# Strassen down projection: other places for the activations' sums, and low parts of plain weight blocks made by an accumulating DMA

## The chip, the cores and the metric

One NeuronCore of a Trainium2 chip runs the whole kernel in one launch. TensorE (PE) multiplies, PEld is its weight load, VectorE (DVE) and ScalarE (ACT) do elementwise work, GpSimd (POOL) does a little more of it, and SyncE (SP) issues the DMAs. The metric is the device time of one execution in microseconds, lower is better. Before the change it is 2497.34 us, the median of three runs (2496.92 to 2497.78).

## What is computed

```python
def swiglu(x, w_gate, w_up, w_down):
    return (jax.nn.silu(x @ w_gate) * (x @ w_up)) @ w_down

for layer in range(2):
    h = h + 0.5 * swiglu(rms_norm(h, norm_ffn1[layer]), ...)
    hn = rms_norm(h, norm_mix[layer])
    h = h + (even_mixer(hn, ...) if layer % 2 == 0 else fourier_mixer(hn, ...))
    h = h + 0.5 * swiglu(rms_norm(h, norm_ffn2[layer]), ...)
return rms_norm(h, norm_final)[:, N_META:]
```

The model width is 1024, the feed-forward width D_FF = 2816. There are 528 + 272 = 800 tokens (two sequences, 16 meta tokens before each). All is float32. Four feed-forward networks (f = 0 to 3) are most of the work: f = 0, the even mixer (attention and pooling), f = 1, f = 2, the odd mixer (a Fourier transform), f = 3.

## The kernel before, in words

**Split products.** A float32 operand is held as a high part (rounded to fp32r) and a low part (the rest), and a product is three matmuls: high by high, high by low, low by high (L1983 to L1985 in gate and up, L2056 to L2058 in down). A weight block of 128x512 is a *unit*: ACT writes its high part (L805) into one of NS = 6 slots, DVE subtracts it from the source and writes the low part (L1215) into the same slot of `w_lo`. A unit's slot is free when PE has done unit n - 6 (`unit_done`).

**Strassen.** Gate, up and most of down are done by Strassen's scheme in Winograd's form: seven products P1, P5, P6, P3, P7, P2, P4 (in this order) in place of eight. Their weights are A11, S1, S2, S4, S3, A12, A22. The four S are sums that DVE makes (L1199 to L1207) from the quarters in `raw`, which SP loads by DMA (a ring of six quarters, 256 KB each); the three A are quarters as they are. Each product is one unit of 12 matmuls. Their right sides are the *forms* B11, T1, T2, B22, T3, B21, N4, with T1 = B12 - B11, T3 = B12 - B22, T2 = B22 - T1, N4 = B21 - T2.

**Chunks.** D_FF is 22 tiles of 128, in chunks of 4, 4, 4, 4 and 6. For each of the first four chunks PE does the gate and up products of its tiles (seven units each; the first two tiles of a network, the lead, are done plainly), and then its down projection in two groups g = 0, 1 of seven units (`down_group`). This change of stage, from the last gate and up unit of a chunk to its first down unit, occurs 4 x 4 = 16 times and is called the *transition* here. The last chunk and the mixers' projections are plain (L1904, L1897).

**The activations.** DVE multiplies up by silu(gate) into `act32` (L1404, L1415), makes the sums T1, T3, T2, N4 there (L1429), ACT writes their high parts (L914) to `act_hi`, DVE their low parts (L1439) to `act_lo`. `act32` and `act_lo` are the same memory, by places 0 to 6 (`ACT_AT`): each low part overwrites the float32 form at its own place, so it waits until the last sum that reads that form is made. B22, T2 and T3 stand side by side and get their high and low parts in one instruction of three forms, which waits for N4; and N4 needs B21, which needs the up half P4, the last gate and up unit of the chunk. For the last tile of a chunk the product is made in halves (L1415): first B22's (half 1), later B21's (half 0).

**The order** of each engine is written out by hand in `ffn`. Between its other steps an engine calls `weights_to(k)`: ACT makes high parts up to unit k + 4, DVE low parts up to k + 3 and sums up to two further. After each half of a down product DVE adds PSUM to `h` (`down_adds`, L1464); PE waits for that add before it accumulates on the same bank again. POOL has nothing to do in a network but one small power (`rstd`). SP's load over an old quarter waits for that quarter's last low part and last sum.

## Time and profile before

| | |
|---|---|
| median of three runs | 2497.34 us |
| the profiled execution | 2500.72 us, of which the span from its first to its last instruction is 2498.9 us |
| PE busy | 2404.6 us, 96% |
| DVE busy | 1987.6 us, 80% |
| ACT busy | 1087.5 us, 44% |
| POOL busy | 80.0 us, 3% |
| DMA | 169.68 MB, one queue of 22.7% of 16 engines |

Busy times are sums of recorded durations; matmuls overlap (they start every 0.18 us and each is recorded as 0.34 us long), so PE's share says only how seldom it stood still. The page's span is 1.8 us shorter than the execution.

### The profile page before, as it was taken

What the parts mean: (1) busy time and instruction counts of PE and PEld (TensorE: products, weight loads), DVE (VectorE), ACT (ScalarE), POOL (GpSimd) and SP (SyncE); (2) the same over time, 40 slices, a digit from 0 to 9 for tenths busy, and PEclk for the clock granted to TensorE, in tenths of its full rate; (3) what the DMA queues carried; (4) which work ended last, traced back from release to release, by engine and by line L of the source; (5) the groups of instructions that cost most, each with busy time, mean ns of one, the idle gap of its engine ahead of it and who ended that gap; (6) DMA issues with size and microseconds to landing.
All of it is one profiled execution on the core that took longest, in us unless ns stands there. A gap on an engine that the chain in (4) does not pass through costs nothing.

```text
span 2498.9 us, 36765 instructions
## 1 busy us (share of the span) xinstructions
PE 2404.6 (96%) x13364; PEld 2348.6 (94%) x13364; DVE 1987.6 (80%) x3664; ACT 1087.5 (44%) x2028; POOL 80.0 (3%) x86
## 2 busy tenths in 40 slices
PE   9999999999999999999999999999999999999998
PEld 8899999999579999999999999999989899999997
DVE  8988988753746988978768897897755898898876
ACT  6453453431743443443444344344443544344353
POOL 0000000006000000000000000000012100000000
PEclk9999999999999999999999999999999999999999
DMA  3222222222011222222221222222221222222223
GB/s 122 68 68 68 68 68 68 72 88 72 18 30 51 60 68 68 66 69 65 68 72 51 68 59 68 68 62 68 76 72 45 78 62 68 70 66 73 70 68 122
DMA packets 92338, 169.68 MB, mean 68 GB/s; under 512 B 10624, under 2 KB 23296, under 8 KB 92032
## 3 DMA queue, kind: packets, MB, share of 16 engines
q1 hardware_dynamic: 92160, 167.34, 22.7%
q8 instruction: 108, 1.77, 0.3%
q14 instruction: 70, 0.57, 0.1%
HBM read 164.02 MB, written 3.28 MB: 67 GB/s over the span
## 4 chain that ended last, share of the span: by engine, by line
PE 76%; DVE 16%; issue 6%; ACT 1%; DMA 0%; POOL 0%; DVEq 0%; SPq 0%; POOLq 0%; ACTq 0%
PE banks L1904 13%; PE banks L1984 12%; PE banks L1985 12%; PE banks L1983 12%; PE banks L2056 6%; PE banks L2058 6%; PE banks L2057 6%; PE banks L2002 3%; PE banks L1897 3%; DVE w_lo L1215 3%; DVE act_lo L1439 2%; DVE act L1429 1%; DVE w_sum L1207 1%; DVE w_sum L1205 1%; PE banks L2185 1%
## 5 line engine op out<-in xcount | busy, mean ns | idle before, releaser
L1984 PE MATMUL banks<-xf_lo,w_hi 128*128 128x400 f32 (+2 forms) x2240 | 767.3, 343 | 0.0
L1983 PE MATMUL banks<-xf_hi,w_hi 128*128 128x400 f32 (+2 forms) x2240 | 764.7, 341 | 2.1 <-ACT p L1005 2.1
L1985 PE MATMUL banks<-xf_hi,w_lo 128*128 128x400 f32 (+2 forms) x2240 | 765.4, 342 | 0.0
L805 ACT ACTIVATE w_hi<-w_sum 128x512 fp32r<-128x512 f32 x464 | 288.1, 627 | 444.7 <-DVE w_sum L1199 170.6
L1983 PEld LDWEIGHTS banks<-xf_hi,w_hi 128*128 128x128 f32 x2240 | 420.4, 188 | 2.7 <-issue 2.7
L1985 PEld LDWEIGHTS banks<-xf_hi,w_lo 128*128 128x128 f32 x2240 | 422.5, 189 | 0.0
L1984 PEld LDWEIGHTS banks<-xf_lo,w_hi 128*128 128x128 f32 x2240 | 420.6, 188 | 0.0
L2056 PE MATMUL banks<-act_hi,w_hi 128*128 128x400 f32 (+2 forms) x896 | 315.3, 352 | 49.5 <-issue 33.2
L1215 DVE TENSOR_TENSOR w_lo<-raw,w_hi 128x512 fp32r<-128x512 f32 (+2 forms) x492 | 329.1, 676 | 17.2 <-ACT w_hi L805 17.0
L805 ACT ACTIVATE w_hi<-raw 128x512 fp32r<-128x512 f32 (+2 forms) x492 | 288.7, 599 | 111.6 <-PE banks L1904 72.4
L1215 DVE TENSOR_TENSOR w_lo<-w_sum,w_hi 128x512 fp32r<-128x512 f32 x464 | 319.0, 694 | 0.7 <-ACT w_hi L805 0.7
L2058 PE MATMUL banks<-act_hi,w_lo 128*128 128x400 f32 (+2 forms) x896 | 311.0, 347 | 0.0
L2057 PE MATMUL banks<-act_lo,w_hi 128*128 128x400 f32 (+2 forms) x896 | 310.8, 347 | 0.0
L1464 DVE SCALAR_TENSOR_TENSOR h<-banks,h 128x400 f32<-128x400 f32 (+4 forms) x624 | 249.3, 461 | 6.1 <-PE banks L2058 5.5
L2056 PEld LDWEIGHTS banks<-act_hi,w_hi 128*128 128x128 f32 x896 | 172.6, 193 | 62.9 <-issue 37.1
L2057 PEld LDWEIGHTS banks<-act_lo,w_hi 128*128 128x128 f32 x896 | 172.9, 193 | 0.1
L2058 PEld LDWEIGHTS banks<-act_hi,w_lo 128*128 128x128 f32 x896 | 172.6, 193 | 0.0
L1199 DVE TENSOR_TENSOR w_sum<-raw 128x512 f32<-128x512 f32 x112 | 77.4, 691 | 67.2 <-PE banks L1985 67.1
L914 ACT ACTIVATE act_hi<-act 128x400 fp32r<-128x400 f32 (+5 forms) x160 | 103.7, 658 | 49.7 <-DVE act L1429 37.1
L1439 DVE TENSOR_TENSOR act_lo<-act,act_hi 128x400 fp32r<-128x400 f32 (+5 forms) x160 | 115.3, 730 | 3.3
L997 ACT ACTIVATE g<-banks 128x400 f32<-128x400 f32 (+2 forms) x80 | 40.0, 500 | 162.5 <-PE banks L1985 162.5
L1019 ACT ACTIVATE up<-banks 128x400 f32<-128x400 f32 (+2 forms) x80 | 40.0, 500 | 160.2 <-PE banks L1985 160.2
(219 smaller groups left out, 3333.1 us busy)
## 6 DMA issues: line engine op xcount, KB each, us to landing
raw<-gate_up_dram SPq DMA_DIRECT2D x352, 256.0 KB, 3.3
raw<-down_dram SPq DMA_DIRECT2D x128, 256.0 KB, 3.4
raw<-down_rest_dram SPq DMA_DIRECT2D x80, 192.0 KB, 2.4
raw<-w_in_dram SPq DMA_DIRECT2D x20, 256.0 KB, 3.4
raw<-w_fourier_dram SPq DMA_DIRECT2D x8, 576.0 KB, 3.7
raw<-w_out_dram SPq DMA_DIRECT2D x16, 256.0 KB, 3.2
h<-x_dram SPq DMA_DIRECT2D x8, 400.0 KB, 7.9
y_dram<-h SPq DMA_DIRECT2D x16, 200.0 KB, 1.9
```

The source lines that it names most:

```text
L805: A.activation(w_hi[:, n % NS, 0:u.cols], source, ACT.Copy).then_inc(w_hi_done, 1)
L914: A.activation(act_hi[:, forms, k, 0:C], act32[:, forms, k, 0:C], ACT.Copy).then_inc(act_hi_done, 1)
L1215: V.tensor_tensor(w_lo[:, n % NS, 0:u.cols], source, as32(w_hi[:, n % NS, 0:u.cols]), ALU.subtract).then_inc(w_ready, 1)
L1439: V.tensor_tensor(act_lo[:, forms, k, 0:C], act32[:, forms, k, 0:C], as32(act_hi[:, forms, k, 0:C]), ALU.subtract).then_inc(act_ready, 1)
L1464: last = V.scalar_tensor_tensor(h[:, m, t:t + n], banks[:, bank, c0:c0 + n], 0.5, h[:, m, t:t + n], ALU.mult, ALU.add)
L1904: ins = M.matmul(banks[:, bank + half, 0:cols], a, b[:, half * cols:(half + 1) * cols], start=first and j == 0, stop=last and j == 2)
L1983: M.matmul(out, a_hi, b_hi, start=fresh and k == 0, stop=False, skip_group_check=True)
L1984: M.matmul(out, a_hi, b_lo, start=False, stop=False, skip_group_check=True)
L1985: ins = M.matmul(out, a_lo, b_hi, start=False, stop=k == KP - 1, skip_group_check=True)
L2056: M.matmul(out, a_hi, b_hi, start=fresh and k == 0, stop=False, skip_group_check=True)
L2057: M.matmul(out, a_hi, b_lo, start=False, stop=False, skip_group_check=True)
L2058: ins = M.matmul(out, a_lo, b_hi, start=False, stop=k == 1, skip_group_check=True)
```

## The change

1. **Places.** The float32 forms get places of their own (`ACT32_AT`): T1 is at 5, and T2 at 6 (over B12, later N4 over T2), while their low parts go to 2 and 5. T2's high and low part become an instruction of their own (`ACT_FORMS` has six names), the pair B22, T3 one of two forms, and neither waits for N4. T1's low part waits for no sum and is made before the transition. The up half of P4, the product B21, the sum N4 and its low part move from before the first down product to behind its third.
2. **Low parts by DMA.** For every unit whose kind begins with A, but for the four of the very first tile, ACT writes the negative of the high part to `w_lo` (one more ACTIVATE, L849 of the new kernel), and POOL issues a DMA (L737) that reads the same quarter from DRAM once more and adds it to `w_lo`. DVE's low part goes. These units come 1.5 places earlier in ACT's order. PE waits for the DMA's semaphore, one for each slot. SP no longer waits for DVE's low part of such a quarter but for ACT's high part.
3. Buffer `n4` moves into `act32`.

Counted over the whole program: DVE issues 592 low parts of weights in place of 956, ACT 364 negatives more, POOL 364 DMAs of 256 KB more; `act_hi` and `act_lo` get 192 instructions each in place of 160. PE's and SP's instructions stay as they are but for their waits.

```diff
-ACT_AT = {"B11": 0, "B21": 1, "T1": 2, "B22": 3, "T2": 4, "T3": 5, "N4": 6, "B12": 6}
+ACT_AT = {"B11": 0, "B21": 1, "T1": 2, "B22": 3, "T3": 4, "T2": 5, "N4": 6}
+ACT32_AT = {"B11": 0, "B21": 1, "B12": 6, "B22": 3, "T1": 5, "T3": 4, "T2": 6, "N4": 6}
-ACT_FORMS = ("B11", "T1", "B22", "B21", "N4")
+ACT_FORMS = ("B11", "T1", "T2", "B22", "B21", "N4")
+TAKEN_BY = {"B11": "T1", "T2": "T2", "B22": "T2", "B21": "N4"}
...
+LOW_BY_DMA = [n for n, u in enumerate(W_UNITS) if u.kind[0] == "A" and n >= GU[0][1]]
+def due(n):
+    return n - 1.5 if n in LOW_AT else n
+HI_ORDER = sorted(range(N_UNITS), key=due)
...
+        def low_parts(a, b):
+            for n in range(a, b):
+                if n in LOW_AT:
+                    u = W_UNITS[n]
+                    pool.wait_ge(negative_done, NEGATIVE_AT[n])
+                    pool.dma_start(w_lo[:, n % NS, 0:u.cols], source(LOADS[u.of[u.kind]].what),
+                                   accum_op=ALU.add).then_inc(low_made[n % NS], 16)
...
@@ weight_hi (ACT)
             if n >= NS:
                 act.wait_ge(unit_done, n - NS + 1)
+            if n in LOW_AT:
+                A.activation(w_lo[:, n % NS, 0:u.cols], source, ACT.Copy, scale=-1.0).then_inc(negative_done, 1)
             A.activation(w_hi[:, n % NS, 0:u.cols], source, ACT.Copy).then_inc(w_hi_done, 1)
...
@@ ffn (ACT), the last tile of a chunk
                         if split:
+                            act_form_high(J, "T2")
                             act_form_high(J, "B22")
-                            weights_to(n0 + 7)
+                            for q in range(3):
+                                weights_to(DS[f][c][0] + q)
                             act_form_high(J, "B21")
+                            weights_to(DS[f][c][0] + 3)
                             act_form_high(J, "N4")
...
@@ ffn (DVE), the last tile of a chunk
                     if last and split:
                         product_half(j, J, 1)
                         act_sum(j, J, "T3")
                         act_sum(j, J, "T2")
-                        act_form_low(j, "T1")
-                        up_first(j, J)
-                        product_half(j, J, 0)
-                        act_sum(j, J, "N4")
-                        act_form_low(j, "B22")
+                        weights_to(n0 + 7)
+                        act_form_low(j, "T2")
...
@@ ffn (DVE), down
                             if g == 0 and q == 2:
-                                act_form_low(last_tile, "B21")
-                            if g == 0 and q == 3:
-                                act_form_low(last_tile, "N4")
+                                act_form_low(j, "B22")
+                            elif g == 0 and q == 3:
+                                up_first(j, J)
+                                product_half(j, J, 0)
+                            elif g == 0 and q == 4:
+                                act_form_low(j, "B21")
+                            elif g == 0 and q == 5:
+                                act_form_low(j, "N4")
                             if g or q:
                                 weights_to(DS[f][c][g] + q)
+                            if g == 0 and q == 3:
+                                act_sum(j, J, "N4")
...
@@ PE
+        def weights_ready(n):
+            if n in LOW_AT:
+                pe.wait_ge(w_hi_done, HI_AT[n])
+                pe.wait_ge(low_made[n % NS], 16 * LOW_AT[n])
+            else:
+                pe.wait_ge(w_ready, LO_AT[n])
```

DVE at the transition of f = 1, chunk 0, before: from the product half that makes B22 to the two adds of the first down product. `act` is the float32 form, `act_lo` its low part, `h<-banks` an add of `down_adds`.

```order
L1415 TENSOR_TENSOR act<-up,g 128x400 [waits up2_scaled,silu_half]
L1429 TENSOR_TENSOR act<-act 128x400 [waits prod_half]
L1429 TENSOR_TENSOR act<-act 128x400 [waits act_summed,prod_half]
L1439 TENSOR_TENSOR act_lo<-act,act_hi 128x400 [waits act_summed,act_hi_done]
L1383 TENSOR_TENSOR up<-banks,rstd 128x400 [waits unit_done]
L1415 TENSOR_TENSOR act<-up,g 128x400 [waits up1_done,silu_done]
L1429 TENSOR_TENSOR act<-act 128x400 [waits act_summed,prod_done]
L1439 TENSOR_TENSOR act_lo<-act,act_hi 128x3x400 [waits act_summed,act_hi_done]
L1464 SCALAR_TENSOR_TENSOR h<-banks,h 128x400 [waits down_part]
L1464 SCALAR_TENSOR_TENSOR h<-banks,h 128x400 [waits unit_done]
```

The same place now:

```order
L1468 TENSOR_TENSOR act<-up,g 128x400 [waits up2_scaled,silu_half]
L1485 TENSOR_TENSOR act<-act 128x400 [waits prod_half]
L1485 TENSOR_TENSOR act<-act 128x400 [waits act_summed,prod_half]
L1265 TENSOR_TENSOR w_lo<-w_sum,w_hi 128x512 [waits w_hi_done]
L1496 TENSOR_TENSOR act_lo<-act,act_hi 128x400 [waits act_summed,act_hi_done]
L1521 SCALAR_TENSOR_TENSOR h<-banks,h 128x400 [waits down_part]
L1521 SCALAR_TENSOR_TENSOR h<-banks,h 128x400 [waits unit_done]
L1265 TENSOR_TENSOR w_lo<-w_sum,w_hi 128x512 [waits w_hi_done]
L1521 SCALAR_TENSOR_TENSOR h<-banks,h 128x400 [waits down_part]
L1521 SCALAR_TENSOR_TENSOR h<-banks,h 128x400 [waits unit_done]
L1496 TENSOR_TENSOR act_lo<-act,act_hi 128x2x400 [waits act_summed,act_hi_done]
```

The single low part is now T2's, four instructions fewer stand ahead of the adds, and the pair of B22 and T3 comes behind the adds of P5.

ACT at the same place, before: from the silu of the first half (`g<-g`) to the high part of B21 and N4.

```order
L1034 ACTIVATE g<-g 128x400 [waits scaled]
L914 ACTIVATE act_hi<-act 128x3x400 [waits act_summed]
L805 ACTIVATE w_hi<-w_sum 128x512 [waits unit_done,sum_made]
L914 ACTIVATE act_hi<-act 128x400 [waits prod_done]
L914 ACTIVATE act_hi<-act 128x400 [waits act_summed]
```

and now:

```order
L1081 ACTIVATE g<-g 128x400 [waits scaled]
L959 ACTIVATE act_hi<-act 128x400 [waits act_summed]
L959 ACTIVATE act_hi<-act 128x2x400 [waits act_summed]
L849 ACTIVATE w_lo<-raw 128x512 [waits unit_done,raw_full5]
L850 ACTIVATE w_hi<-raw 128x512
L850 ACTIVATE w_hi<-w_sum 128x512 [waits unit_done,sum_made]
```

The high part of the sum S3 (the last row) stood right behind the forms; a negative (`w_lo<-raw`) and a high part now stand between.

ACT at the start of the same chunk's last tile, before: the copy of P1's bank, the silu of the tile before, a high part, the copy of P5's bank (`p<-banks`), for which P3 waits.

```order
L997 ACTIVATE g<-banks 128x400 [waits prod_done,unit_done]
L895 ACTIVATE g<-g 128x800 [waits scaled]
L805 ACTIVATE w_hi<-raw 128x512 [waits unit_done,raw_full1]
L1005 ACTIVATE p<-banks 128x400 [waits up2_done,unit_done]
L805 ACTIVATE w_hi<-raw 128x512 [waits unit_done,raw_full0]
```

and now:

```order
L1043 ACTIVATE g<-banks 128x400 [waits prod_done,unit_done]
L940 ACTIVATE g<-g 128x800 [waits scaled]
L849 ACTIVATE w_lo<-raw 128x512 [waits unit_done,raw_full0]
L850 ACTIVATE w_hi<-raw 128x512
L1051 ACTIVATE p<-banks 128x400 [waits up2_done,unit_done]
```

One negative more stands ahead of the copy.

## Rows read from the trace of the kernel before

**Rows 1.** The page, part 1: busy time of each engine.

```profile
PE 2404.6 (96%) x13364; PEld 2348.6 (94%) x13364; DVE 1987.6 (80%) x3664; ACT 1087.5 (44%) x2028; POOL 80.0 (3%) x86
```

**Rows 2.** Waits of PE: us in total, times, longest.

```profile
PE banks L2056 <- issue: 33.2, 22, 2.0
PE banks L2056 <- DVE act_lo L1439: 16.1, 16, 1.6
PE banks L2002 <- DVE w_lo L1215: 4.7, 3, 2.7
...
PE banks L1983 <- ACT p L1005: 2.1, 2, 1.0
```

**Rows 3.** PE in order of time, transition of f = 1, chunk 0.

```profile
1039.56 0.34 PE L2056 MATMUL banks<-act_hi,w_hi 128*128 128x400 f32 x1
...
1042.13 0.34 PE L2058 MATMUL banks<-act_hi,w_lo 128*128 128x400 f32 x1
1043.24 0.45 PE L2056 MATMUL banks<-act_hi,w_hi 128*128 128x400 f32 x1 [0.78 <-DVE act_lo L1439]
...
1044.80 0.34 PE L2058 MATMUL banks<-act_hi,w_lo 128*128 128x400 f32 x1
1047.06 0.58 PE L2056 MATMUL banks<-act_hi,w_hi 128*128 128x400 f32 x1 [1.92 <-issue]
...
1050.45 0.41 PE L2057 MATMUL banks<-act_lo,w_hi 128*128 128x400 f32 x1
```

**Rows 4.** DVE in order of time, the same place.

```profile
1034.56 0.69 DVE L1202 TENSOR_TENSOR w_sum<-w_sum,raw 128x512 f32<-128x512 f32 x1
1035.16 0.68 DVE L1215 TENSOR_TENSOR w_lo<-raw,w_hi 128x512 fp32r<-128x512 f32 x1
...
1038.55 0.57 DVE L1651 TENSOR_TENSOR g<-banks,g 128x400 f32<-128x400 f32 x1
1039.15 0.58 DVE L1654 TENSOR_TENSOR g<-g,rstd 128x400 f32<-128x400 f32 x1
...
1043.11 0.57 DVE L1383 TENSOR_TENSOR up<-banks,rstd 128x400 f32<-128x400 f32 x1
...
1045.07 1.41 DVE L1439 TENSOR_TENSOR act_lo<-act,act_hi 128x1200 fp32r<-128x1200 f32 x1
1046.39 1.05 DVE L1464 SCALAR_TENSOR_TENSOR h<-banks,h 128x400 f32<-128x400 f32 x2
```

**Rows 5.** ACT in order of time, the tile before the transition and the transition.

```profile
1020.08 0.50 ACT L1019 ACTIVATE up<-banks 128x400 f32<-128x400 f32 x1 [2.83 <-PE banks L1985]
...
1028.21 0.87 ACT L895 ACTIVATE g<-g 128x800 f32<-128x800 f32 x1 [1.06 <-DVE g L1611]
1028.99 0.62 ACT L805 ACTIVATE w_hi<-raw 128x512 fp32r<-128x512 f32 x1
1029.51 0.48 ACT L1005 ACTIVATE p<-banks 128x400 f32<-128x400 f32 x1
...
1042.54 1.21 ACT L914 ACTIVATE act_hi<-act 128x1200 fp32r<-128x1200 f32 x1 [2.25 <-DVE act L1429]
```

**Rows 6.** Windows with granted clock (PEclk, third from the end): first and last transition with a fall.

```profile
187.00:191.00 4.00, 4.00 (x16) 3.99 (x15) 4.00 (x12) 0.00 (x0) 0.00 (x0) 0.57 0.00 0
2317.00:2321.00 4.00, 4.00 (x16) 4.00 (x16) 4.00 (x13) 0.00 (x0) 0.00 (x0) 0.58 0.00 0
```

**Rows 7.** DMA: the queue's share of 16 engines, and us from issue to landing.

```profile
q1 hardware_dynamic: 92160, 167.34, 22.7%
raw<-gate_up_dram SPq DMA_DIRECT2D x352, 256.0 KB, 3.3
h<-x_dram SPq DMA_DIRECT2D x8, 400.0 KB, 7.9
```

**Rows 8.** DVE's low parts (L1215), 565 to 610 us, beside POOL's pooling: ns min/median/max.

```profile
L1215 DVE TENSOR_TENSOR w_lo<-raw,w_hi x12: 677/684/2061, 565.8 to 608.8; 128x512 fp32r<-128x512 f32 x12
```

**Rows 9.** Windows in a network: PE, PEld, DVE, ACT busy.

```profile
1400.00:1500.00 100.00, 97.30 (x525) 96.65 (x525) 86.56 (x149) 42.47 (x76) 0.00 (x0) 0.98 0.22 64
```

More of the change, by code:

```diff
@@ L213, in plan_strassen @@
         W_UNITS.append(Unit(kind, of, 0, QUARTER))
-    for name in ("A11", "A21"):
-        LAST_SUM[of[name]] = SUM_AT[first + WEIGHT_OF.index("S3")]
+    for name, kind in (("A11", "S3"), ("A21", "S3"), ("A22", "S1"), ("A12", "S4")):
+        LAST_SUM[of[name]] = SUM_AT[first + WEIGHT_OF.index(kind)]
     return first
@@ L263 @@
 N_UNITS = len(W_UNITS)
+LOW_BY_DMA = [n for n, u in enumerate(W_UNITS) if u.kind[0] == "A" and n >= GU[0][1]]
+LOW_AT = {n: sum(1 for o in LOW_BY_DMA[:i + 1] if o % NS == n % NS) for i, n in enumerate(LOW_BY_DMA)}
+NEGATIVE_AT = {n: i + 1 for i, n in enumerate(LOW_BY_DMA)}
+def due(n):
+    return n - 1.5 if n in LOW_AT else n
+HI_ORDER = sorted(range(N_UNITS), key=due)
+HI_AT = {n: i + 1 for i, n in enumerate(HI_ORDER)}
+LO_AT, _n = [], 0
+for _u in range(N_UNITS):
+    _n += _u not in LOW_AT
+    LO_AT.append(_n)
 TILES = ((0, 2, 4, 6, 1, 3, 5, 7),) + (tuple(range(KD)),) * (N_FFN - 1)
@@ L472, in build @@
     w_ready = sem("w_ready")
+    negative_done = sem("negative_done")
+    low_made = [sem(f"low_made{s}") for s in range(NS)]
     table_hi = sem("table_hi")
@@ L701, in then, with network @@
             pool.wait_ge(pool_chain, chain[0])
-        power(norm_of("ffn1_0"))
+        def low_parts(a, b):
[5 more added lines that the diff above has]
+                                   accum_op=ALU.add).then_inc(low_made[n % NS], 16)
+        def network(f, name):
+            first = GU[f][0] + (6 if f in EARLY else 8)
+            low_parts(GU[f][0], first)
+            power(norm_of(name))
+            low_parts(first, DN[f][0])
+        network(0, "ffn1_0")
         pool.wait_ge(unit_done, WIN[0])
@@ L738, in _ @@
             pool.wait_ge(pooled_done, g + 1)
-        power(norm_of("ffn2_0"))
-        power(norm_of("ffn1_1"))
+        network(1, "ffn2_0")
+        network(2, "ffn1_1")
         pool.wait_ge(unit_done, WF[0])
@@ L777, in _ @@
                 fold(m + 1)
-        power(norm_of("ffn2_1"))
+        network(3, "ffn2_1")
         for half in range(2):
@@ L1212, in weight_lo @@
             u = W_UNITS[n]
-            dve.wait_ge(w_hi_done, n + 1)
-            source = raw_cols(u) if u.kind in ("raw", "A11", "A12", "A21", "A22") else w_sum[:, n % NS, 0:u.cols]
+            dve.wait_ge(w_hi_done, HI_AT[n])
+            source = raw_cols(u) if u.kind[0] != "S" and u.kind not in ("even", "odd") else w_sum[:, n % NS, 0:u.cols]
             V.tensor_tensor(w_lo[:, n % NS, 0:u.cols], source, as32(w_hi[:, n % NS, 0:u.cols]),
@@ L1224, in weights_to @@
                     summed[0] += 1
-                weight_lo(made[0])
+                if made[0] not in LOW_AT:
+                    weight_lo(made[0])
                 made[0] += 1
@@ L1401, in product @@
                 else:
-                    at = slice(ACT_AT["B21"], ACT_AT["B22"] + 1, 2) if t % 2 else slice(0, ACT_AT["B12"] + 1, 6)
+                    if j == LEAD:
+                        dve.wait_ge(form_ready, N_FORM * (f + 1))
+                    at = slice(ACT32_AT["B21"], ACT32_AT["B22"] + 1, 2) if t % 2 else slice(0, ACT32_AT["B12"] + 1, 6)
                     out, a, b = act32[:, at, t // 2, 0:C], two(up[:, 0:W]), two(gate[j % 2][:, 0:W])
@@ L1414, in product_half @@
                     dve.wait_ge(up1_done, J + 1)
-                V.tensor_tensor(act32[:, ACT_AT["B22" if half else "B21"], 1, 0:C], up[:, cols],
+                V.tensor_tensor(act32[:, ACT32_AT["B22" if half else "B21"], 1, 0:C], up[:, cols],
                                 gate[j % 2][:, cols], ALU.mult).then_inc(prod_half if half else prod_done, 1)
@@ L2050, in down_group @@
                             if g == 0 and mu == 0:
-                                part = "B22" if form in ("T2", "T3") else form
+                                part = "B22" if form == "T3" else form
                                 pe.wait_ge(act_ready, act_at(f, c, k, part))
@@ L2304, in _ @@
             n = WF[m]
-            pe.wait_ge(w_ready, n + 1)
+            weights_ready(n)
             for g in range(4):
```

88 lines of the change are left out of this document (50 added, 38 removed).

## Prediction

> **What bounds the kernel now.** I read the shares first: PE is busy 96% of the span [rows 1], so a change can only win what PE loses. DVE at 80% and ACT at 44% matter only where PE waits for them. Then the waits of PE: the first two lines are at L2056, the first matmul of a down product. They hold 33.2 + 16.1 = 49.3 us in 38 waits; nothing else in the networks comes near (the next that lies in every network is 2.1 us for ACT's copy of P5's bank) [rows 2]. Then PE in order of time at one transition [rows 3]: one step from matmul to matmul is 2.57 us / 14 = 0.18 us, a unit of 12 is 2.2 us. The second product (T1) waits once, 1042.13 to 1043.24; the third (T2) once more, 1044.80 to 1047.06. From start to start these cost 0.93 and 2.08 us, 0.15 each more than the waits' own numbers. Behind them ten matmuls take 3.39 us (1047.06 to 1050.45) where 1.8 would do: 1.55 us, because the granted clock falls to its lower level, 1.2 of 2.4 GHz. In windows of 4 us this reads 0.57 and 0.58; nine of the 16 transitions show it, of which the first and the last stand in [rows 6].
> So the transitions lose 49.3 + 38 x 0.15 = 55 us in waits and about 9 x 1.5 = 13.5 us by the clock, 68 us together. That is the most that the change can win there.
>
> **Why PE waits there.** DVE is late and its chain is long [rows 4]. Call T0 the start of the first down product, 1039.56. The gate's sum of P2 (L1651) could start when P2 is done, at T0 - 2.2 = 1037.4; it starts at 1038.55. Between 1034.56 and this a low part from `raw` (1035.16) takes 0.6 of the queue. The three-form low part ends at 1045.07 + 1.41 = 1046.5, and PE resumes at 1047.06.
>
> **Change, part 1: low parts leave DVE.** 364 low parts at 0.60 us in the queue (1034.56 to 1035.16 is such a step [rows 4]) are 218 us less DVE, so its share in a network's window, 86.6% [rows 9], falls by 9 points. Where DVE is not waited for this is worth nothing. Between tile and transition three go; L1651 then starts on time, 1.15 us earlier.
>
> **Part 2: the sums' places.** I lay the new order of DVE on the old durations, from T0, for f = 1. L1651 at -2.1, its scaling at -1.5, T1's low part at -1.0, sum and low part of weights to +0.7, product half 0.6, T3 0.6, T2 done at 2.4, a low part of weights beside ACT's high part of T2 (0.55), T2's low part at 3.0 to 3.6. PE needs it at 4.4 + 0.55 (the second half of the form is read three matmuls later): the long wait is gone, and so is T1's. Now the next. ACT does T2's high part at 2.5, the pair's at 2.9, then, new, a negative and a high part (0.52 each, 1028.99 to 1029.51 [rows 5]), and only then S3's high part, to 5.4. DVE's low part of S3 stands ahead of the adds of P5, which stand ahead of the pair's low part: adds of P1 to 4.5, wait, S3 5.4 to 6.0, two adds at 0.48, the pair (0.9) at 7.0 to 8.0. PE wants it at 6.6 + 0.55 = 7.15: 0.85 us late. Behind it adds 1.0, `up` 0.6, product 0.6, a weight sum 0.6, N4 0.5, adds 1.0, then B21's low part, done at 12.7; PE wants it at 11.0 + 0.85 + 0.55 = 12.4: 0.3 us late. N4's is in time.
>
> **Part 3: the tile before.** T2's low part now stands ahead of N4's sum, and its high part comes only behind ACT's copy of `up` (1020.08 [rows 5]), that is at 1021.0 to 1021.55. DVE stands still for that, then does low part, N4, two weights, the gate's sum, the pair, two weights, two low parts, `up`, and the scaling, by the same durations to 1028.9. The scaling before let ACT's silu start at 1028.21; it now starts 0.7 later. Silu 0.8, negative 0.5, high part 0.5, then the copy of P5's bank at 1030.75 to 1031.25, where before it was at 1029.51. P3 starts at T0 - 4 x 2.2 = 1030.75 and waits for it: 0.5 us late. This too occurs once in a chunk.
>
> **Part 4: ACT.** 364 negatives at 0.52 in the queue are 190 us more on ACT, 1087.5 to some 1280, 51%. Only the two places above are on the path; elsewhere it waits for PE (2.83 us ahead of the copy at 1020.08 [rows 5]).
>
> **Part 5: the DMAs.** 364 x 256 KB are 95 MB more. The queue's 167.34 MB are 22.7% of 16 engines; at that rate this is 13%, at twice the work for a byte 26%, so the engines stay below half. How long one accumulating DMA from POOL takes, no row shows. The nearest: 3.3 us for a plain 256 KB, 7.9 us for `x` with eight others in flight [rows 7]. I take 4 to 5. PE's slack: a unit's slot comes free five units (11 us) ahead of it. In a plain tile the tightest is A22's: negative done some 4.0 us into the tile, wanted at 6 x 2.2: 9 us. At the transition A12's negative is done at T0 + 4.3 and wanted at 11.0 + 0.85: 7.5 us; in the last tile 7.6. So up to 7.5 us it costs nothing. It can't win anything beside part 1, since PE's only waits for a low part of weights in a network are 4.7 us in three places at L2002, the lead [rows 2], of which at least the first, in the kernel's first tile, stays as it is.
> The Trainium skill (DMA: Bandwidth & Descriptors, Anatomy of one DMA) gives a DMA from GpSimd 2.0 us and its bytes over 436 GB/s, by which 256 KB would be 2.6 us, an estimate; it says nothing there of accumulation. The plain row is 0.7 us above it. By it the DMAs cost nothing, as in the sum.
>
> PE waits for two semaphores at such a unit, where it waited for one; the down products' first matmuls wait for three already and start 0.18 us apart when all have come [rows 3], so 0 (if each of the 364 cost 0.05, 18 us, within the range). SP's shorter waits cost and win nothing, because no engine waits for `raw` in rows 2; nor does the new place of `n4`.
>
> **Part 6: contention.** Beside POOL's pooling one DVE low part took 2061 ns where the median is 684 [rows 8]; so work on POOL can hold DVE up to 1.4 us. I take 0 for issuing a DMA, the median of the same row; the other end is 1.4 for each of three in a tile.
> The Trainium skill (SBUF — State Buffer, Who interferes with whom) says that a DVE instruction with two SBUF inputs contends with a GpSimd instruction that reads SBUF, not with one that only writes it; descriptors are written. [Rows 8] agrees on the first half: pooling reads. By the rule the cost is 0; if the descriptor work reads too, it is the rival below.
>
> **Sum.** Removed 68. New: 0.5 + 0.85 + 0.3 = 1.65 us in the eight transitions of f = 1 and 2, 13 us; in f = 0 and 3 the adds of the second half are cut in two by the sequences, which I put at 0.1 us for each pair: 2.2 us, 18 us. The clock: two falls left, 3 us (between 0 and 9 falls, 0 and 13). 68 - 34 = 34 us. 2500.7 - 34 = 2466.7 in the profiled execution, which is 3.4 above the median of the runs: **2463 us**.
>
> **Rivals.**
> - *The new waits don't come* (ACT finishes S3 earlier than I lay it out). Against it stands the printed order. Then all 68 go: 2429 us.
> - *POOL's descriptor work holds DVE.* With 0.6 us for each DMA DVE gets back what it gave, the transitions lose what they lost less T1's share, 2495; with 1.4 us, 3 x 0.8 = 2.4 us of 15.4 come on top of 86.6%, DVE passes 100% and bounds the networks: 2530. For it: 2061 ns. Against it: the median is untouched in the same stretch.
> - *The accumulating DMA lands late*, the one on the other side. Place: A22's and A12's unit, PE at their first matmul. Up to 7.5 us free; at 8.5 us the last tiles and transitions give back 16 x (1.0 + 0.9) = 30 us, which is about zero gain, the point from which it decides; at 10 us 80 tiles lose 1.0 us and the 16 places 2.4 and 2.5 more: 2463 + 80 + 62 = 2605 us. For it: reading the destination too, 7.9 us of `x`; against it: 3.3 us.
> - *The change takes work off an engine that isn't waited for*: then only part 2 acts, L1651 stays 1.15 late and each wait is longer by as much, 16 x 1.15 = 18 us less gain: 2481. Against it: DVE's rows around 1035 to 1038.5 follow each other without a gap [rows 4], so what is taken out moves the rest forward.
>
> **Chances.** Forecast 0.5, no new waits 0.15, only part 2 0.05, POOL 0.12, late DMA 0.18. Range 2425 to 2520: it leaves out the late DMA above 9 us and DVE bound fully; the forecast's own is 2445 to 2480. A measurement of this kernel can tell 0.2% (5 us) from no change. Faster than 2492: 0.5 + 0.15 + 0.05 + 0.03 = 0.73; within: 0.07 (POOL 0.04, DMA 0.03); slower: 0.20.
>
> **What would show it.** Right: no wait at the second and third down product; one of about 0.9 us at the fourth (P3) for the pair's low part, one of 0.3 at the sixth, one of 0.5 at P3 of a chunk's last tile for ACT's copy; DVE 1740 to 1780 us busy, ACT about 1290; accumulating DMAs landing in 4 to 5 us; DVE's low parts at 0.68 still. Wrong: PE waiting for `w_lo` of a DMA at the first matmul of A12 or A22 units; DVE instructions over 0.9 us for 512 columns wherever POOL issues; the 1.9 us wait still there.

## The result and the profile after

The changed kernel takes 2481.7 us (median of 4 runs, 2481.2 to 2485.8) where the kernel before took 2497.5 on the same chip: ratio 0.9942, 95% interval 0.993 to 0.9955. By the ratio it is faster by 14 us (11 to 17 by the interval; the medians are 16 us apart), well over the 5 us that can be told from no change, and short of the 34 us forecast. The profiled execution took 2481.65 us; the one of before stood 3.2 us above its median, so from span to span the difference is 2498.9 - 2479.8 = 19.1 us, and that is what the stages below add up to.

The page of the changed kernel: busy time of each engine (to be held against [rows 1]), and the queues.

```profile
PE 2400.6 (97%) x13364; PEld 2332.4 (94%) x13364; DVE 1783.9 (72%) x3332; ACT 1272.2 (51%) x2424; POOL 394.7 (16%) x450
...
q1 hardware_dynamic: 92160, 167.34, 24.0%
q0 software_dynamic: 52416, 95.44, 23.3%
...
raw<-gate_up_dram SPq DMA_DIRECT2D x352, 256.0 KB, 4.1
```

DVE gave 204 us away and ACT took 185, close to what was forecast. In the networks this reads as forecast too: DVE's share of a window falls from 86.6% [rows 9] to 77.3% (engines in the order of [rows 9]).

```profile
1400.00:1500.00 100.00, 98.28 (x536) 96.71 (x535) 77.33 (x135) 51.79 (x96) 15.57 (x18) 1.00 0.56 119
```

The waits of PE, which answer to [rows 2] (us in total, times, longest; L2128 is now the first matmul of a down product, L2055 that of gate and up, L1051 ACT's copy of P5's bank):

```profile
PE banks L2128 <- DVE act_lo L1496: 11.7, 24, 0.6
PE banks L2055 <- ACT p L1051: 11.4, 16, 1.8
PE banks L2128 <- issue: 10.9, 20, 1.1
```

The down products' waits fell from 49.3 us in 38 to 22.6 us in 44, none longer than 1.1 where the longest was 2.0. The wait for ACT's copy, which was 2.1 us in two places, is now 11.4 us in 16: one at every last tile of a chunk. Measured from PE's first matmul of a stage to that of the next, the 16 down stages together are 33.4 us shorter, the last tiles of the 16 chunks 16.9 us longer, and the rest of the kernel 2.6 us shorter: 33.4 - 16.9 + 2.6 = 19.1 us.

PE in order of time at the transition of [rows 3] (f = 1, chunk 0; the first down product starts at T0 = 1034.28, and the row at 1025.44 is P3 of the last tile):

```profile
1025.44 0.42 PE L2055 MATMUL banks<-xf_hi,w_hi 128*128 128x400 f32 x1 [0.50 <-ACT p L1051]
...
1034.28 0.34 PE L2128 MATMUL banks<-act_hi,w_hi 128*128 128x400 f32 x1
...
1038.49 0.35 PE L2130 MATMUL banks<-act_hi,w_lo 128*128 128x400 f32 x1
1039.39 0.42 PE L2128 MATMUL banks<-act_hi,w_hi 128*128 128x400 f32 x1 [0.55 <-issue]
...
1041.83 0.42 PE L2128 MATMUL banks<-act_hi,w_hi 128*128 128x400 f32 x1
...
1042.26 0.35 PE L2130 MATMUL banks<-act_hi,w_lo 128*128 128x400 f32 x1
1043.16 0.45 PE L2128 MATMUL banks<-act_hi,w_hi 128*128 128x400 f32 x1 [0.55 <-DVE act_lo L1496]
...
1047.44 0.34 PE L2130 MATMUL banks<-act_hi,w_lo 128*128 128x400 f32 x1
1047.82 0.45 PE L2128 MATMUL banks<-act_hi,w_hi 128*128 128x400 f32 x1
```

A step is 0.18 us, so the reader takes 0.18 off each distance (and the matmul behind a wait is followed 0.26 to 0.29 us later, another 0.1 us lost, called its slow start below): the third product (P6) loses 0.72 at its first matmul, the fourth (P3) 0.22 at its first (1041.83, behind the matmul at 1041.43) and 0.72 at its fourth, the sixth (P2) 0.20 at its fourth. The first three matmuls of a down product read the half of the form that an earlier tile gave, and the next three the half of the last tile. The second product no longer waits, and no clock fall follows any of the 16 transitions, where nine did. DVE at the same place, which answers to [rows 4]:

```profile
1030.64 0.57 DVE L1439 TENSOR_TENSOR up<-up,p 128x400 f32<-128x400 f32 x1 [0.58 <-ACT up L1065]
...
1032.95 0.57 DVE L1709 TENSOR_TENSOR g<-banks,g 128x400 f32<-128x400 f32 x1
...
1038.23 0.58 DVE L1496 TENSOR_TENSOR act_lo<-act,act_hi 128x400 fp32r<-128x400 f32 x1
1038.72 1.05 DVE L1521 SCALAR_TENSOR_TENSOR h<-banks,h 128x400 f32<-128x400 f32 x2
1040.55 0.69 DVE L1265 TENSOR_TENSOR w_lo<-w_sum,w_hi 128x512 fp32r<-128x512 f32 x1 [0.78 <-ACT w_hi L850]
1041.16 1.05 DVE L1521 SCALAR_TENSOR_TENSOR h<-banks,h 128x400 f32<-128x400 f32 x2
1042.12 0.98 DVE L1496 TENSOR_TENSOR act_lo<-act,act_hi 128x800 fp32r<-128x800 f32 x1
```

T2's low part is made by 1038.81 (T0 + 4.5), in time for P6's second half of the form. But P6 also accumulates on the bank that P1 left, and for that it waits until DVE has added it to `h`. That add starts at 1038.72 and is the first of two in 1.05 us; it ends near 1039.3, and PE starts at 1039.39. So the wait at P6 is for P1's add, which stands behind T2's low part, and not for T2: the matmul that waits reads the earlier half of the form. The pair's low part (1042.12) stands behind the low part of S3, for which DVE stood still 0.78 us, and two adds.

The first chunks of the first and the last network (f = 0 and 3) hold a wait of 1.8 us for ACT's copy, and the clock falls behind it. A window at the second of them, in the changed kernel's trace (the length, PE, PEld, DVE, ACT, POOL busy, then the granted clock, third from the end):

```profile
2004.11:2008.11 4.00, 3.86 (x14) 3.89 (x15) 2.20 (x4) 2.46 (x5) 1.12 (x2) 0.60 0.78 140
```

### The profile page after: what moved, and what is told of

The parts are those of the page before. It is cut to its first block, busy times and chain, and to the rows that moved or that the text cites. A ratio compares the mean times of both kernels' runs of the same rounds, so it can differ in the third digit from the quotient of the medians.

```text
span 2479.8 us, 37500 instructions
## 1 busy us (share of the span) xinstructions
PE 2400.6 (97%) x13364; PEld 2332.4 (94%) x13364; DVE 1783.9 (72%) x3332; ACT 1272.2 (51%) x2424; POOL 394.7 (16%) x450
## 3 DMA queue, kind: packets, MB, share of 16 engines
q1 hardware_dynamic: 92160, 167.34, 24.0%
q0 software_dynamic: 52416, 95.44, 23.3%
## 4 chain that ended last, share of the span: by engine, by line
PE 75%; DVE 13%; issue 6%; ACT 5%; DMA 0%; POOL 0%; DVEq 0%; SPq 0%; ACTq 0%; POOLq 0%
PE banks L2055 13%; PE banks L2056 13%; PE banks L2057 13%; PE banks L1969 13%; PE banks L2074 5%; PE banks L2128 5%; PE banks L2130 4%; PE banks L2129 4%; PE banks L1962 3%; DVE act_lo L1496 2%; DVE w_lo L1265 2%; ACT w_hi L850 2%; DVE h L1521 2%; DVE act L1485 1%; DVE w_sum L1257 1%
## 5 line engine op out<-in xcount | busy, mean ns | idle before, releaser
L2055 PE MATMUL banks<-xf_hi,w_hi 128*128 128x400 f32 (+2 forms) x2240 | 767.0, 342 | 11.9 <-ACT p L1051 11.4
L2056 PE MATMUL banks<-xf_lo,w_hi 128*128 128x400 f32 (+2 forms) x2240 | 768.3, 343 | 0.0
L737 POOL DMA_DIRECT2D w_lo<-gate_up_dram x268 | 232.1, 871 | 1378.2 <-ACT w_lo L849 1377.7
L2055 PEld LDWEIGHTS banks<-xf_hi,w_hi 128*128 128x128 f32 x2240 | 421.0, 188 | 17.6 <-DVE w_lo L1265 16.2
L2056 PEld LDWEIGHTS banks<-xf_lo,w_hi 128*128 128x128 f32 x2240 | 421.5, 188 | 0.0
L849 ACT ACTIVATE w_lo<-raw 128x512 fp32r<-128x512 f32 x364 | 227.7, 625 | 215.0 <-PE banks L2057 119.5
L2128 PE MATMUL banks<-act_hi,w_hi 128*128 128x400 f32 (+2 forms) x896 | 311.4, 347 | 23.4 <-DVE act_lo L1496 11.7
L2130 PE MATMUL banks<-act_hi,w_lo 128*128 128x400 f32 (+2 forms) x896 | 305.3, 341 | 0.0
L2129 PE MATMUL banks<-act_lo,w_hi 128*128 128x400 f32 (+2 forms) x896 | 305.2, 341 | 0.0
L1521 DVE SCALAR_TENSOR_TENSOR h<-banks,h 128x400 f32<-128x400 f32 (+4 forms) x624 | 248.4, 448 | 19.1 <-PE banks L2130 18.4
L2128 PEld LDWEIGHTS banks<-act_hi,w_hi 128*128 128x128 f32 x896 | 168.0, 188 | 44.1 <-DVE act_lo L1496 22.5
L959 ACT ACTIVATE act_hi<-act 128x400 fp32r<-128x400 f32 (+2 forms) x192 | 106.7, 580 | 110.9 <-DVE act L1485 58.7
L737 POOL DMA_DIRECT2D w_lo<-down_dram x96 | 83.0, 871 | 405.4 <-ACT w_lo L849 402.9
```

The source lines that it names most:

```text
L737: pool.dma_start(w_lo[:, n % NS, 0:u.cols], source(LOADS[u.of[u.kind]].what), accum_op=ALU.add).then_inc(low_made[n % NS], 16)
L849: A.activation(w_lo[:, n % NS, 0:u.cols], source, ACT.Copy, scale=-1.0).then_inc(negative_done, 1)
L1521: last = V.scalar_tensor_tensor(h[:, m, t:t + n], banks[:, bank, c0:c0 + n], 0.5, h[:, m, t:t + n], ALU.mult, ALU.add)
L2055: M.matmul(out, a_hi, b_hi, start=fresh and k == 0, stop=False, skip_group_check=True)
L2056: M.matmul(out, a_hi, b_lo, start=False, stop=False, skip_group_check=True)
L2128: M.matmul(out, a_hi, b_hi, start=fresh and k == 0, stop=False, skip_group_check=True)
```

## The experiments

All were run against the kernel before. Ratios are to it, with the 95% interval. Where two of the kernels are held against each other, the distance can differ by 2 us between ratios and medians, and the text says which of them it takes. The first two take the change apart.

**Places only.** All low parts stay on DVE; the new places of the sums and of their forms' parts are kept.

```
-LOW_BY_DMA = [n for n, u in enumerate(W_UNITS) if u.kind[0] == "A" and n >= GU[0][1]]
+LOW_BY_DMA = []
```

> The changed kernel without any accumulating DMA: DVE makes all low parts again, as before the change; the sums' places and the new order of DVE and ACT stay. Theory A (places and relief of DVE both count: the new order needs the time that the DMAs free on DVE): the gate's sum of P2 comes about 1.2 us later than in the changed kernel, so the add of P1 and the pair's low part are later; the three PE waits at the third and fourth down product and at P3 of the last tile stay or grow (1 to 2 us each). Down stages still some 1 us shorter each than before, last tiles 1 to 2 us longer: 2490 us, between 2485 and 2505. Theory B (the gain comes from the places alone, the DMAs are neutral): 2481 us, as the changed kernel.

Measured: 2503.6 us, ratio 1.0020 (1.0011 to 1.0028): slower than before. The long waits become two middling ones at each transition, and they cost as much: from stage to stage the 16 down stages are only 3.8 us shorter than before, and the last tiles 6.2 us longer.

```profile
PE banks L2128 <- issue: 25.3, 16, 1.7
PE banks L2128 <- DVE act_lo L1496: 23.9, 26, 1.5
```

**DMAs only.** The kernel before, with the accumulating DMAs and the shorter waits of SP's loads, and the sums where they were.

```
+LOW_BY_DMA = [n for n, u in enumerate(W_UNITS) if u.kind[0] == "A" and n >= GU[0][1]]
...
+                    pool.wait_ge(negative_done, NEGATIVE_AT[n])
+                    pool.dma_start(w_lo[:, n % NS, 0:u.cols], source(LOADS[u.of[u.kind]].what),
+                                   accum_op=ALU.add).then_inc(low_made[n % NS], 16)
```

> The kernel before with the accumulating DMAs alone: places, three-form instruction and order as before, low parts of A units by DMA. Theory A: DVE is 1.15 us earlier at a transition, so each of the 16 transitions loses about 1 us less and fewer have the fall of the clock: 2475 to 2485 us; PE's wait for the copy of P5's bank stays small, since T2's high part is not split off. Theory B (the DMAs are neutral): 2497 us. Theory C (the DMAs cost: landing late or POOL holding DVE): above 2500 us.

Measured: 2488.6 us, ratio 0.9963 (0.9949 to 0.9976). The six runs lie between 2481.3 and 2494.1 us, and the profiled one is the fastest of them, so its waits are the least that this kernel shows; in it the clock still falls behind seven of the 16 transitions. T1's wait shrinks to 0.61 to 0.75 us; the wait of 2 us at the third product stays at all 16 transitions, since its chain starts behind the last gate and up unit:

```profile
PE banks L2105 <- issue: 30.6, 16, 2.0
PE banks L2105 <- DVE act_lo L1481: 8.3, 16, 0.6
```

So the parts are not additive: +5 us and -9 us by themselves, -14 together, by the ratios.

**The copy first.** In every gate and up tile ACT makes its copy of P5's bank ahead of the negative and the high part that stood before it.

```
-                    weights_to(n0 + 1)
...
                     A.activation(p5[:, 0:C], banks[:, SUM53, 0:C], ACT.Copy).then_inc(copied, 1)
+                    weights_to(n0 + 1)
```

> The changed kernel with one step of ACT moved: in every gate and up tile the copy of P5's bank comes ahead of the negative and high part of A22 instead of behind them. Theory A (the 11.4 us of waits for this copy, and the two falls of the clock behind the 1.8 us waits, come from ACT's order): 13 last tiles win 0.7 us, the first chunks' 1.0 us, and the clock 3 us: about 13 us less, 2469 us. Theory D (DVE's late scaling alone makes them, since silu itself is late): the waits go down by no more than 0.3 each, 2478 us.

Measured: 2476.2 us, ratio 0.9914 (0.9902 to 0.9927), 7 us better than the change by the ratios, 5.5 by the medians. The waits for the copy are gone but for two (2.3 us), yet the gate and up stages (with the plain tiles at their start) are still 10 us longer than before. New waits stand where PE needs A22's low part: ten of them, 3.4 us in all, end within 0.1 us of the landing of that unit's own DMA. Fifteen more, 3.5 us in all, stand at P7, for ACT's next copy. One of the ten, PE and then POOL and ACT at the same place:

```profile
1124.80 0.34 PE L2057 MATMUL banks<-xf_hi,w_lo 128*128 128x400 f32 x1
1125.52 0.42 PE L2055 MATMUL banks<-xf_hi,w_hi 128*128 128x400 f32 x1 [0.38 <-issue]
```

```profile
1119.33 0.86 POOL L737 DMA_DIRECT2D w_lo<-gate_up_dram  x1 [5.80 <-ACT w_lo L849]
```

```profile
1117.80 0.62 ACT L849 ACTIVATE w_lo<-raw 128x512 fp32r<-128x512 f32 x1
```

The negative that moved behind the copy is ready at 1118.4, its DMA is issued at 1119.33 and lands 6.1 us later, at 1125.43, which is when PE goes on. The margin that I took for 7.5 us and more is used up.

**T2's high part earlier.** In the third tile of a chunk ACT makes T2's high part ahead of its copy of `up`, not behind it.

```
                     weights_to(n0 + 4)
+                    if t == 2 and split:
+                        act_form_high(J - 1, "T2")
...
-                        act_form_high(J - 1, "T2")
```

> The changed kernel with T2's high part of the third tile of a chunk made by ACT ahead of its copy of up (where ACT stands still for 3 us) instead of behind it. Theory A (DVE's 1.3 us wait for that high part delays the scaling of the next tile, and with it silu and the copy of P5's bank): DVE is 1.3 us earlier, the waits for the copy go from 0.5-0.8 us to 0 in 14 tiles and shrink in the two first chunks: 10 to 13 us less, 2470 us. Theory D' (the two ACT instructions ahead of the copy are the cause whatever DVE does): 2481 us.

Measured: 2468.7 us, ratio 0.9882 (0.9869 to 0.9895), 15 us better than the change by the ratios, 13 by the medians. The gate and up products of each chunk take as long as before the change (within 0.05 us), the waits for the copy are gone but for two of 0.4 us, in the first chunks of the first and the last network, and with them the falls of the clock: the window of 4 us behind the copy in the first chunk of f = 3, which read 0.60 in the change, now reads 1.00:

```profile
1996.50:2000.50 4.00, 4.00 (x25) 4.00 (x24) 3.37 (x7) 1.83 (x5) 0.86 (x1) 1.00 0.95 197
```

The down stages keep their 32.6 us. What the copy waited for was DVE's scaling, which was late because DVE had stood still for T2's high part.

**The adds first.** The last one, and besides: P1's adds ahead of T2's low part and of the weights, and the pair's low part ahead of S3's.

```
                         act_sum(j, J, "T2")
-                        weights_to(n0 + 7)
+                        down_adds(c, 0, 0)
                         act_form_low(j, "T2")
+                        weights_to(n0 + 7)
```

> On top of e4 (T2's high part early), DVE's order at the transition: the two adds of P1 right behind T2's sum, then T2's low part, then the weights; and the pair's low part ahead of the low part of S3. Theory A (the two waits left at the transition are for the adds of P1 standing behind T2's low part, and for the pair's low part standing behind S3's, which waits for ACT): the adds end at T0 + 3.8 (wanted at 4.4), the pair at 7.2 (wanted at 7.1), so both waits (0.7 us each in f = 1 and 2, 0.9 and 0.75 in f = 0 and 3) go but for 0.1; B21's low part, at 12.4, is then wanted at 11.5, so 0.9 us comes back at the sixth product: net 0.6 to 0.9 us for each of 16 chunks, 10 to 14 us less than e4, 2456 to 2459 us. Theory E (the first wait is for something else, a weight's DMA or T2's low part): the first wait stays and the gain is under 5 us, 2464 to 2469 us.

Measured: 2454.0 us, ratio 0.9824 (0.981 to 0.9837), 14.6 us better than the last by the medians. The 14.0 us that the down stages win are the balance of four places: the third product takes 11.8 us less over the 16 transitions, the fourth 12.6 less, the sixth 9.6 more and the seventh 1.2 more. Two things were moved in one run, and what each gave the fourth product was not separated. The waits put down to "issue" at the down products are gone: of the three groups in the change's waits one is left.

```profile
PE banks L2130 <- DVE act_lo L1497: 13.9, 24, 0.9
```

At the same transition DVE and PE now read:

```profile
1027.90 1.05 DVE L1522 SCALAR_TENSOR_TENSOR h<-banks,h 128x400 f32<-128x400 f32 x2
1028.87 0.57 DVE L1497 TENSOR_TENSOR act_lo<-act,act_hi 128x400 fp32r<-128x400 f32 x1
...
1030.91 0.98 DVE L1497 TENSOR_TENSOR act_lo<-act,act_hi 128x800 fp32r<-128x800 f32 x1
```

```profile
1036.26 0.34 PE L2132 MATMUL banks<-act_hi,w_lo 128*128 128x400 f32 x1
1037.22 0.45 PE L2130 MATMUL banks<-act_hi,w_hi 128*128 128x400 f32 x1 [0.62 <-DVE act_lo L1497]
```

The third product starts in time; what is left here is 0.78 us at the sixth, for B21's low part.

**B21's part first.** N4's sum and B21's low part directly behind the last half product.

```
                                 product_half(j, J, 0)
-                            elif g == 0 and q == 4:
+                                act_sum(j, J, "N4")
                                 act_form_low(j, "B21")
```

> e5, and N4's sum and B21's low part right behind B21's product, ahead of a weight sum and of the adds of P3. Theory A: B21's low part ends at T0 + 11.0 instead of 12.4, before it is wanted (11.5), so the sixth product waits for nothing and the transition loses 0.2 us in all: another 0.6 to 0.9 us for each chunk, 2445 us (between 2440 and 2450). Theory F (DVE as a whole is the bound of the first down group, so a wait only moves to the next product): the same time as e5.

Measured: 2457.0 us, ratio 0.9836 (0.9823 to 0.9849): 3 us worse than the last one by the medians. The intervals overlap, but the down stages of the profiled executions are 3.3 us longer too. The wait for `act_lo` goes from 13.9 to 1.3 us, and two others come in its place at the seventh product, for a high part of weights by ACT and for an accumulating DMA:

```profile
PE banks L2128 <- ACT w_hi L850: 9.7, 12, 1.0
...
PE banks L2128 <- DMA w_lo<-down_dram: 4.6, 4, 1.6
```

**No head start.** The kernel with T2's high part earlier, but ACT makes negative and high part of a block in the order of the units, not 1.5 units ahead.

```
-    return n - 1.5 if n in LOW_AT else n
+    return n
```

> e4 with the A units in their plain order on ACT (due = n instead of n - 1.5), so the negatives of gate and up tiles are made some 1.5 units (3 us) later. Theory G (the accumulating DMAs, 6 to 8 us from issue to landing, are hidden only by a thin margin): PE waits at the first matmul of A12 and A22 units of most tiles, 0.2 to 2 us each: 20 to 100 us more than e4, 2490 to 2570 us. Theory H (they have several us of slack, as predicted: 7.5 us free against a landing of 4 to 5): no change, 2468 us.

Measured: 2477.4 us, ratio 0.9916 (0.9902 to 0.9929), 9 us worse than with the head start by the medians, against the 20 us and more that I had put down. New waits stand at gate and up units (L2056 here):

```profile
PE banks L2056 <- issue: 13.8, 26, 2.0
PE banks L2056 <- ACT w_hi L850: 6.9, 6, 1.9
```

```profile
936.85 0.45 PE L2056 MATMUL banks<-xf_hi,w_hi 128*128 128x400 f32 x1 [1.98 <-issue]
```

They are waits for accumulating DMAs, though the view calls most of them "issue". The row at 936.85 is the first matmul of an A22 unit; that unit's DMA was issued at 928.18 and landed at 936.76. In the same way 39 waits at A22 units of gate and up tiles, 26 us in all, end within 0.1 us of the landing of the unit's own DMA; in the same kernel with the head start none does. The gate and up stages lose 29.5 us to it but the down stages win 28.8 against the same kernel with the head start, being 30 to 32 us long. That DVE catches up while PE stands at A22, just ahead of the transition, would explain the gain; it is argued, not shown. What the two kinds of stage lose and win does not add up to the 9 us of the medians (the profiled executions differ by 6, and the rest lies in other stages).

**The best order without DMAs.** The kernel with the adds first, all low parts on DVE. This is the question that the first two left: is the relief of DVE needed once the order is right?

```
-LOW_BY_DMA = [n for n, u in enumerate(W_UNITS) if u.kind[0] == "A" and n >= GU[0][1]]
+LOW_BY_DMA = []
```

> The order of e5_adds_first, but all low parts made on DVE again (as in e1_places_only). Theory P, DVE's relief is needed at the transitions whatever the order, because three low parts of weights more stand ahead of T2's there: the distance from e1_places_only to the changed kernel (2503.6 - 2481.7 = 22 us) stays, and this kernel takes about 2454 + 22 = 2476 us, with waits for act_lo of over 1.2 us again. Rival Q, what e1_places_only lost was lost to the same two misplaced steps, and once they are put right DVE at 80% is enough: 2454 to 2460 us, and the accumulating DMAs are worth next to nothing.

Measured: 2496.4 us, ratio 0.9990 (0.9982 to 0.9999). The DMAs are worth 42 us here by the medians, more than either theory said; all of it (41.9 us) lies in the 16 down stages, 1.8 to 3.7 us each.

```profile
PE banks L2130 <- DVE act_lo L1497: 32.6, 32, 2.0
```

At one transition of f = 1, first DVE and then PE: a low part from `raw` stands again between the last half product and B21's low part (another, at 953.40, ahead of them), 0.6 us each in the queue. PE waits 1.92 us, and the clock falls behind it (0.54 us for one matmul at 959.92, where 0.34 is the rule):

```profile
956.73 0.69 DVE L1266 TENSOR_TENSOR w_lo<-raw,w_hi 128x512 fp32r<-128x512 f32 x1
...
958.78 0.57 DVE L1497 TENSOR_TENSOR act_lo<-act,act_hi 128x400 fp32r<-128x400 f32 x1
```

```profile
957.30 0.34 PE L2132 MATMUL banks<-act_hi,w_lo 128*128 128x400 f32 x1
959.40 0.45 PE L2130 MATMUL banks<-act_hi,w_hi 128*128 128x400 f32 x1 [1.77 <-DVE act_lo L1497]
...
959.92 0.54 PE L2132 MATMUL banks<-act_hi,w_lo 128*128 128x400 f32 x1
```

**More head start.** The kernel with the adds first, with 2.5 units in place of 1.5.

```
-    return n - 1.5 if n in LOW_AT else n
+    return n - 2.5 if n in LOW_AT else n
```

> e5_adds_first with a head start of 2.5 units for blocks whose low part comes by DMA, where it had 1.5. Theory G, the margin of the DMAs is thin (e7_no_head_start lost 9 us without a head start): what is left of it in e5_adds_first goes, some 1 to 4 us, 2450 to 2453 us. Rival H, in e5_adds_first no product waits for a DMA any more, and a longer head start only puts the high parts of sums, which PE wants sooner, behind two passes of 0.52 us on ACT: S3's and the like are later by about 1 us at 16 transitions and some last tiles, 2465 to 2475 us.

Measured: 2492.8 us, ratio 0.9979 (0.997 to 0.9988), 38 us worse. Rival H had the direction, not the place. The down stages are unchanged (-1.1 us in all), S3 is not late; the 38 us lie in the gate and up stages. PE waits 0.28 to 0.34 us at nearly all of the 80 tiles (1.0 to 1.5 at the first tile of each network), where PE needs the bank of the gate's P1 and ACT copies it only behind one more negative and high part. With the slow starts this is 35 us of the 38:

```profile
PE banks L2057 <- ACT g L1043: 7.0, 39, 0.4
```

```profile
886.70 0.63 ACT L849 ACTIVATE w_lo<-raw 128x512 fp32r<-128x512 f32 x1 [0.51 <-PE banks L2059]
887.23 0.62 ACT L850 ACTIVATE w_hi<-raw 128x512 fp32r<-128x512 f32 x1
887.75 0.62 ACT L850 ACTIVATE w_hi<-w_sum 128x512 fp32r<-128x512 f32 x1
888.28 0.48 ACT L1043 ACTIVATE g<-banks 128x400 f32<-128x400 f32 x1
```

Theory G was right about the DMAs and wrong about the price: no wait of PE ends with a DMA's landing any more, where in the kernel with the adds first five did, 1.6 us in all. So the head start is bounded from both sides, and 1.5 lies between two losses, of 9 us (in the order before the adds were moved) and of 38 us.

The medians (us), by who makes the low parts of blocks that are no sums:

| order of the activations' parts | DVE | accumulating DMA | worth of the DMAs |
|---|---|---|---|
| before | 2498 | 2488.6 | 9 |
| changed | 2503.6 | 2481.7 | 22 (19 by the ratios) |
| changed, T2's high part and the adds put right | 2496.4 | 2454.0 | 42 |

## Why the prediction was wrong in size

The forecast was 34 us less and about half of it came: 14 by the ratio, 16 by the medians, 19 between the profiled executions. 2481.7 us lies in the range of 2425 to 2520, but outside the 2445 to 2480 that went with the forecast itself.

**The bound and its places: right.** PE at 96%, the loss at the transitions, the 2 us wait of the third product and the clock behind it: the fall at nine transitions went away with the long wait, as the sum had it.

**Part 1 (DVE's relief): it acts, but the step that I gave for it failed.** The gate's sum of P2 was to start at T0 - 2.1, 1.15 us earlier than before. It started at T0 - 1.3 (1032.95), against T0 - 1.0 before: 0.3 us earlier in f = 1 and 2, 0.5 to 1.0 in f = 0 and 3. I had argued that DVE's rows there follow each other without a gap, so that what is taken out moves the rest forward. It does so only up to DVE's next wait: the row at 1030.64 shows DVE standing still 0.58 us for ACT's copy of `up`, and ACT in turn makes that copy behind PE:

```profile
1030.11 0.50 ACT L1065 ACTIVATE up<-banks 128x400 f32<-128x400 f32 x1 [2.07 <-PE banks L2057]
```

At all 16 transitions DVE now waits there (0.54 to 0.78 us), and before at none. The kernel with the DMAs only has the gate's sum at the same T0 - 1.3. "Where DVE is not waited for this is worth nothing" holds in plain tiles. At a transition it is waited for all along: the same 364 low parts are worth 9, 22 or 42 us, by what else the order leaves in the way. I had priced them by the three that stood ahead of the gate's sum, and not those behind T0.

**Part 2 (the sums' places): the term that was mis-sized most.** I wrote "the long wait is gone" and put P6's wait at nothing, because T2's low part would be made at T0 + 3.6. P1's adds I put at "to 4.5" without holding them against P6, which needs the first of them at T0 + 4.4. Laid out, the first add ended at about T0 + 4.15, 0.25 us of margin. In fact T2's low part started at T0 + 3.95 in place of 3.0, most of it because of the gate's sum above; the add ended near T0 + 5.0, and P6 waited 0.72 us (0.5 to 1.3 in f = 0 and 3), 14 us in all with the slow starts. Whether a T2 part on time would have been enough was not run; that the add is what P6 waits for, the kernel with the adds first shows: its first add ends at T0 + 3.8, T2's low part starts at T0 + 4.2, 0.3 us later than in the changed kernel, and P6's first matmul no longer waits.

The row was there: PE resumed at 1047.06 in [rows 3], and T2's low part had ended at 1046.5 in [rows 4]; the 0.55 us between are the first half of the adds that start at 1046.39. I took them for the delay of a semaphore. The waiting matmul is P6's first, which reads the earlier half of the form, so T2's part was not what it waited for even then.

The other waits, 0.85 forecast for the pair and 0.3 for B21, measured 0.72 and 0.20 (0.75 and 0.5 in f = 0 and 3). That the pair's fits is partly luck: its low part started at T0 + 7.8 in place of 7.0, and PE, held up at P6, came to it 1.0 us later than laid. P3 also waits 0.2 to 0.3 us at its first matmul, for P5's add, some 5 us in all; the sum had nothing for it. With the slow starts, all new waits of the down products are about 40 us where the sum had 23, and about 73 went where it had 68. For the 16 down stages together I forecast 68 - 26 = 42 us less and 33.4 came.

**Part 3 (the tile before): right in place and cause, too small in size.** Forecast 0.5 us at each of the 16 last tiles, 8 us; by their lengths they lost 0.73 in f = 1 and 2, 0.85 to 1.3 in f = 0 and 3, and 2.7 us in the first chunk of these two networks, where a clock fall follows. That is 16.9 us. I forecast two falls left, at transitions; two were left, here, so that the number agrees is luck. With T2's high part put earlier the whole term went. Of the 15 us by which the sum missed the profiled gain, 8.6 are part 2 and 8.9 part 3, less 2.6 that the rest of the kernel won.

**Part 4 (ACT): right.** 1272 us where 1280 was given.

**Part 5 (the DMAs): the size wrong, the conclusion right for the changed kernel only.** I took 4 to 5 us; they land in 4.1 to 9.7 us, median 6.2. Up to 7.5 us was to cost nothing. In the changed kernel two waits of PE end within 0.1 us of the landing of their unit's DMA: 1.7 us in the plain tiles of f = 3 (at 1948.58) and 0.34 us at an A22 unit (at 2105.00). At the A22 units of gate and up tiles 2.1 us were left at the median between landing and PE's first matmul, where 9 us free and a landing of 4 to 5 would leave 4 to 5. So in three experiments PE waited for more of them: with the copy first and with no head start, which make negatives later, and with B21's part first, which brings PE to the block sooner. The Trainium skill (DMA: Bandwidth & Descriptors, Anatomy of one DMA) would give 2.6 us, an estimate from its fit for a plain transfer; the least of 364 here was 4.1, so the measurement decides against using it for an accumulating one.

The landing times, in the profile of the changed kernel, of the 364 DMA issues by POOL (ns min/median/max of the issue; the last line is us to landing):

```profile
L737 POOL DMA_DIRECT2D w_lo<-gate_up_dram x268: 862/862/1214, 19.8 to 2401.4; - x134
...
DMA to landing us min/median/max: 4.1/6.2/9.7
```

**Part 6 (contention): right.** DVE's low parts of sums took 685 ns at the median beside 364 issues, 686 before; the 2060 ns of [rows 8] come again, and all nine low parts over 0.8 us lie in the mixers, beside an elementwise instruction of POOL; none lies beside an issue. By the rule of the Trainium skill (SBUF — State Buffer, Who interferes with whom), that a DVE instruction with two SBUF inputs contends with a GpSimd instruction that reads SBUF and not with one that only writes it, this was to be expected for descriptors, which are written, and the traces agree.

**The rivals.** "No new waits" and "POOL holds DVE" are refuted by the rows above. "Only part 2 acts" gave 2481, the number that was measured, and that is luck: places alone took 2503.6 us, and part 1 does act (22 us between places only and the change); what brought the time there is P6's and the copy's waits. The late DMA costs 2 us in the changed kernel; that its margin is thin is what the rival had right.

The best kernel of the study is the one with the adds first: 2454.0 us, 0.9824 of the kernel before and 28 us under the changed one.

## What to carry to other kernels

When a wait goes, list every condition of the waiting instruction and when each is met, not only the one that came last: here the add of a bank stood 0.5 us behind the low part that seemed to be the releaser. Work taken off a busy engine and work put in another order can be worth more together than apart (here 14 us together, 9 and -5 apart), so try the two together before either is dropped. A transfer in a chain of hand-overs needs its margin counted against its slowest landing, since every reordering upstream spends some of it; and giving it more room on an in-order engine is paid by what stands behind.

## What the hardware showed that was not expected

An accumulating DMA of 256 KB from POOL into on-chip memory lands in 6.2 us at the median where a plain load of that size from SP took 3.3 us before [rows 7], and 4.1 us beside them. For its 95.44 MB it holds the 16 engines for 23.3% of the span, where 167.34 MB of plain loads hold them 24.0%: 1.7 times the engine time for a byte. POOL is held 0.86 us by each issue. They queue behind each other: no two of the 364 land less than 1.2 us apart, and where five were issued within 7.2 us, from 1939.74 on, they landed 2.0 us apart, 7.7 to 9.7 us behind their issue. None of this slowed DVE. Why one takes 4.1 us at the least was not measured by itself.
